# Two of the four weight-block sums of each summed unit are made by GpSimd instead of VectorE

## The chip, the core and the metric

The kernel runs on one core of one Trainium2 chip. A core has five engines that run their own instruction streams and meet only at semaphores: TensorE (PE, the matmuls; PEld is its weight load), VectorE (DVE), ScalarE (ACT), GpSimd (POOL) and SyncE (SP, which here only issues DMAs). The metric is the device time of one execution in microseconds. Three executions of the kernel before took 2109.12, 2109.4 and 2110.14 us; the median is 2109.4.

## The reference, cut to what matters

Two decoder layers over 256 tokens of width 2048: an RG-LRU and dilated attention mixer, then an MLP; a differential attention mixer, then an MLP. All arrays are float32. The change touches only the MLPs:

```python
def squared_relu_mlp(x, w1, w2):      # w1: 2048 x 8192, w2: 8192 x 2048
    h = jax.nn.relu(x @ w1)
    return (h * h) @ w2
x = layer_norm(ALPHA * x + squared_relu_mlp(x, mlp_w1[layer], mlp_w2[layer]), ...)
```

## The kernel before, in words

**Three products for one.** Each float32 operand is cut in two: a rounded part "hi" (ScalarE copies it to fp32r) and the rest "lo" (VectorE subtracts hi from the original). A product is then three matmuls, hi by hi, hi by lo and lo by hi (`three_products`, lines 1101 to 1103). So every weight that arrives by DMA passes through ScalarE and then VectorE before TensorE can use it.

**The turns.** An MLP takes its 16 strips of 512 hidden columns in pairs. The first pair and the last strips are made apart; the other six pairs are six *turns* (`pair_step`), five in a hardware loop and one behind it. There are twelve turns in the kernel, six in each layer. A turn first multiplies x by two strips of w1 (the up half), then turns and squares the hidden values and multiplies an earlier pair by w2 (the down half, 16 chunks). The up half consists of eight *units* of 1 MB of w1 each: two K tiles by two strips, which is four blocks of 128x512, in the order w_12, w_11, w_22, w_21. `UNITS = "SSOSOSSO"`: units 0, 1, 3, 5 and 6 are *summed*, the others ordinary.

**A summed unit** uses seven block products instead of eight, as in Strassen's scheme. Three work on blocks as they came (`plain_products`, 9 matmuls), four on sums of blocks (`summed_products`, 12 matmuls). The sums are T_1 = w_12 - w_11 and T_3 = w_12 - w_22 (one instruction, line 2046, 128x1024), then T_2 = w_22 - T_1 and T_4 = w_21 - T_2 (two instructions, line 2050, 128x512 each). T_4 needs T_2, and T_2 needs T_1. The four sums lie in `w_sums[e % 2]`, which is the tile `late` for the summed units 0, 3 and 6 and part of `rg` for units 1 and 5.

**The path of a summed unit, number u.** The DMA lands. VectorE makes the four sums (`weight_sums`, parts 0, 1, 2). ScalarE makes hi of the three plain blocks (`plain_hi`, line 860) and, when all four sums are there, hi of the sums (`summed_hi`, line 868). VectorE makes lo of the plain blocks in place in `raw` (`plain_lo`, line 2023), which must wait until the last sum has read them, and then lo of the sums in place (`summed_lo`, line 2030). TensorE waits for `s_plain_lo` before the plain and for `s_lo` before the summed products. Ordinary units and the down half have a simpler path: `chunk_hi` (line 854), `chunk_lo` (line 2010), two chunks of 128x1024 a unit.

**What sets the order.** Nothing is scheduled by a program: each engine's order is the order of the calls in its own `pair_step`. Weights land in four slots (`raw`) used in a ring; the lo parts are made in place there, so the load of a unit (SP, line 417) waits on `s_used` until TensorE has used the unit four before it, and for a summed one until its plain products are done. SP also issues small DMAs that move turned blocks (line 411) in between. VectorE adds finished down products to the residual in the same queue (`add_down`, line 1608), which waits for TensorE.

**GpSimd** does almost nothing: a memset and small loads at the start, four pairs of loads of the gain and bias rows of the layer norms (line 533) and, at the very end, part of the last layer norm (lines 539 and 541). The lines to follow are quoted here:

Of the kernel before, what the change touches and what calls it, by code (L numbers as in the profile page):

```python
# [34 lines left out]
P = 128  # L35
# [169 lines left out]
def build(nc, x, positions, ev_w_in, ev_conv_w, ev_conv_b, ev_gate_a_w, ev_gate_a_b, ev_gate_x_w,  # L205
# [12 lines left out]
    with ExitStack() as ctx:  # L218
# [3 lines left out]
        def sem(name):  # L222
            return ctx.enter_context(nc.semaphore(name))
# [106 lines left out]
        s_sums, s_sum_hi, s_sum_lo = sem("x_sums_made"), sem("x_sums_hi"), sem("x_sums_lo")  # L330
        s_wsum = sem("weight_sums_made")
        s_relu = sem("hidden_cut_at_zero")
        s_plain_hi, s_plain_lo = sem("plain_blocks_hi"), sem("plain_blocks_lo")
        s_prod, s_copied, s_final = sem("products_joined"), sem("first_product_copied"), sem("pair_completed")
        s_dve, s_pool = sem("vector_step"), sem("gpsimd_step")
# [21 lines left out]
        def raw_unit(k):  # L357

            q = k % BLK // 2
            return raw[:, 2 * q:2 * q + 2].rearrange("p k t c -> p (k t c)")  # L360

        def sum_cell(j, e, h):

# [141 lines left out]
        def _(pool):  # L505
# [16 lines left out]
                    pool.dma_start(gates_w[64 * half:64 * half + 64, n, :, 64 * half:64 * half + 64], src).then_inc(s_gw, 16)  # L522


            for n in range(4):
                if n == 0:
                    pool.wait_ge(s_yalo, 2)
                elif n == 2:
                    pool.wait_ge(s_gained, GROUPS * n)
                else:  # L530
                    pool.wait_ge(s_used, ((B_M0, B_M1)[n // 2] + 2 * FB - 2) * BLK)
                for i, row in enumerate(ln_rows(n)):
                    pool.dma_start(gain_bias[:, i], row.partition_broadcast(P)[:, 0, :]).then_inc(s_gb, 16)
# [11 lines left out]
        def _(act):  # L545
# [279 lines left out]
            def mlp(n, b0):  # L825
# [37 lines left out]
                def summed_hi(blk, u, turn):  # L863

                    e = SUMMED.index(u)
                    act.wait_ge(s_wsum, turn * (3 * NS) + (3 * e + 3))
                    act.wait_ge(s_used, blk * BLK + (RING_PRIOR[2 * u + 1] + 1))
                    nc.scalar.activation(hi_part(RING_CELL[2 * u + 1], 4), w_sums[e % 2], ACT.Copy).then_inc(s_hi, 2)

# [637 lines left out]
        def _(dve):  # L1507
# [478 lines left out]
            def mlp(n, b0, n0):  # L1986
# [32 lines left out]
                def plain_lo(blk, u, turn):  # L2019

                    dve.wait_ge(s_plain_hi, turn * NS + (SUMMED.index(u) + 1))
                    dve.wait_ge(s_wsum, turn * (3 * NS) + (3 * SUMMED.index(u) + 3))
                    nc.vector.tensor_tensor(lo_part(2 * u, 1, 3), raw_unit(2 * u)[:, CN:4 * CN],
                                            hi_part(RING_CELL[2 * u], 3).bitcast(F32), ALU.subtract).then_inc(s_plain_lo, 1)

# [4 lines left out]
                    nc.vector.tensor_tensor(w_sums_lo[e % 2], w_sums[e % 2], hi_part(RING_CELL[2 * u + 1], 4).bitcast(F32),  # L2030
                                            ALU.subtract).then_inc(s_lo, 2)

                def weight_sums(blk, u, turn, part):

                    e = SUMMED.index(u)
                    w_12, w_11, w_22, w_21 = (raw_unit(2 * u)[:, j * CN:j * CN + CN] for j in range(4))
                    t = [w_sums[e % 2][:, j * CN:j * CN + CN] for j in range(4)]
                    if part == 0:  # L2040
                        dve.wait_ge(s_raw[u % PAIRS], (blk + u // PAIRS) * 16)
                        if e >= 2:
                            dve.wait_ge(s_used, blk * BLK + (2 * SUMMED[e - 2] + 2))
                        pair = w_sums[e % 2][:, 0:2 * CN].rearrange("p (a c) -> p a c", a=2)
                        w_2, w_1 = (raw_unit(2 * u).rearrange("p (a c) -> p a c", a=4)[:, a:b] for a, b in ((0, 1), (1, 3)))
                        nc.vector.tensor_tensor(pair, w_2.to_broadcast([P, 2, CN]), w_1, ALU.subtract).then_inc(s_wsum, 1)
                    else:
                        dve.wait_ge(s_wsum, turn * (3 * NS) + (3 * e + part))
                        out, a, b = ((t[T_2], w_22, t[T_1]), (t[T_4], w_21, t[T_2]))[part - 1]
                        nc.vector.tensor_tensor(out, a, b, ALU.subtract).then_inc(s_wsum, 1)  # L2050

                def add_down(blk, q, nb, k):

# [83 lines left out]
                def pair_step(i, last=False):  # L2137
# [5 lines left out]
                    def lo(k):  # L2143
                        chunk_lo(blk, k, RING_CELL[k])

                    def sums(u, part):
                        weight_sums(blk, u, turn, part)

                    sums(0, 0)
                    add_down(blk, i, 2, -4)  # L2150
                    sums(0, 1)
                    sums(0, 2)
                    plain_lo(blk, 0, turn)
                    sums(1, 0)
                    summed_lo(blk, 0)
                    sums(1, 1)
                    sums(1, 2)
# [3 lines left out]
                    sums(3, 0)  # L2161
                    lo(4)
                    sums(3, 1)
                    lo(5)
                    sums(3, 2)
                    plain_lo(blk, 3, turn)
                    summed_lo(blk, 3)
                    sums(5, 0)
                    lo(8)
                    sums(5, 1)  # L2170
                    lo(9)
                    sums(5, 2)
                    plain_lo(blk, 5, turn)
                    sums(6, 0)
                    summed_lo(blk, 5)
                    sums(6, 1)
                    sums(6, 2)
                    plain_lo(blk, 6, turn)
                    summed_lo(blk, 6)
                    lo(14)  # L2180
# [172 lines left out]
```

## Time and profile before

| | |
|---|---|
| median of three executions | 2109.4 us |
| the profiled execution, its own time | 2108.34 us |
| its span, first to last instruction | 2106.6 us |
| TensorE busy | 2087.9 us, 99% |
| VectorE busy | 1628.7 us, 77% |
| ScalarE busy | 1098.6 us, 52% |
| GpSimd busy | 25.6 us, 1% |
| granted TensorE clock, mean | 0.998 |

The span is 1.74 us shorter than the execution's own time, and that execution is 1.06 us below the median. A timeline row merges neighbours that are alike; its duration runs from the first start to the last end. The row of a matmul is 0.39 us long but the next starts 0.227 us after it, since they overlap in the array; the pace is read from the starts. Likewise one VectorE instruction starts some 0.08 us before the one ahead of it has ended.

### The profile page before, as it was taken

Reading aid. Unit: us, or ns where it says so; the run is one execution under the profiler, and the core shown is the slowest. Engines: PE = TensorE matmul, PEld = TensorE weight load, DVE = VectorE, ACT = ScalarE, POOL = GpSimd, SP = SyncE. Lnnn points to the kernel's source line nnn. Section 1 sums busy time; section 2 is a strip of 40 time slices with the busy share of each in tenths; the row PEclk is TensorE's granted clock in tenths of the full one; section 3 lists DMA queues with packets and bytes.
Section 4 is the critical chain, followed back from the end, with each engine's and each line's share of the span. In section 5 each row is a group of like instructions: output and inputs, shape, how many; then the busy total and the mean of one; then the engine's idle time right before and its main releaser. Section 6 shows DMA issues by size and latency. Waiting matters only on the chain.

```text
span 2106.6 us, 26918 instructions
## 1 busy us (share of the span) xinstructions
PE 2087.9 (99%) x9824; PEld 1747.5 (83%) x9824; DVE 1628.7 (77%) x1647; ACT 1098.6 (52%) x1246; POOL 25.6 (1%) x38
## 2 busy tenths in 40 slices
PE   9999999999999999999999999999999999999997
PEld 8888887888888888888888888888888888888886
DVE  6766667869789798896687767577698978978866
ACT  5445656445555455454645554555354554645643
POOL 2000000000000000000000000000000000000001
PEclk9999999999999999999999999999999999999999
DMA  9554574566666666667564555454666666676664
GB/s 288 184 177 160 169 247 164 185 205 211 219 210 227 208 205 217 208 220 272 166 221 159 181 178 179 162 198 155 207 218 209 213 222 203 211 229 198 228 202 178
DMA packets 216122, 426.19 MB, mean 202 GB/s; under 512 B 14992, under 2 KB 50048, under 8 KB 215024
## 3 DMA queue, kind: packets, MB, share of 16 engines
q1 hardware_dynamic: 214208, 415.75, 59.6%
q0 software_dynamic: 1840, 9.44, 1.3%
q8 instruction: 48, 0.79, 0.2%
q14 instruction: 26, 0.21, 0.0%
HBM read 406.26 MB, written 2.10 MB: 194 GB/s over the span
## 4 chain that ended last, share of the span: by engine, by line
PE 96%; DVE 1%; DMA 1%; ACT 1%; POOL 0%; issue 0%; POOLq 0%; ACTq 0%
PE ps L1101 20%; PE ps L1103 20%; PE ps L1102 20%; PE ps L1013 10%; PE ps L1039 6%; PE ps L1041 6%; PE ps L1040 6%; PE ps L1017 5%; DMA raw<-in_ev_w_in 1%; PE ps L1214 0%; PE ps L1084 0%; PE ps L1255 0%; PE ps L1213 0%; PE ps L1218 0%; DVE w_lo L1513 0%
## 5 line engine op out<-in xcount | busy, mean ns | idle before, releaser
L1513 DVE TENSOR_TENSOR w_lo<-raw,w_hi 128x1024 fp32r<-128x1024 f32 x264 | 319.5, 1218 | 126.0 <-ACT w_hi L554 125.2
L1102 PE MATMUL ps<-raw_lo,yT 128*128 128x512 f32 x944 | 367.2, 389 | 0.0
L554 ACT ACTIVATE w_hi<-raw 128x1024 fp32r<-128x1024 f32 x256 | 267.5, 1056 | 169.9 <-PE ps L1041 114.0
L1013 PE MATMUL ps<-xT,w_hi 128*128 128x512 f32 x1016 | 258.7, 396 | 1.4 <-DVE xT L1558 1.0
L854 ACT ACTIVATE w_hi<-raw 128x1024 fp32r<-128x1024 f32 x168 | 173.7, 1050 | 144.7 <-DMA raw<-in_mlp_w 82.7
L1102 PE MATMUL ps<-raw_lo,xT 128*128 128x512 f32 x548 | 213.2, 389 | 0.0
L1013 PEld LDWEIGHTS ps<-xT,w_hi 128*128 128x128 f32 x1016 | 183.1, 188 | 35.6 <-issue 1.5
L1102 PEld LDWEIGHTS ps<-raw_lo,yT 128*128 128x128 f32 x944 | 177.2, 188 | 36.7
L1101 PE MATMUL ps<-w_hi,yT 128*128 128x512 f32 x508 | 198.0, 390 | 0.1
L1103 PE MATMUL ps<-w_hi,yT 128*128 128x512 f32 x508 | 197.7, 389 | 0.0
L854 ACT ACTIVATE more_hi<-raw 128x1024 fp32r<-128x1024 f32 x116 | 116.8, 1050 | 127.5 <-DMA raw<-in_mlp_w 127.5
L2010 DVE TENSOR_TENSOR raw_lo<-raw,w_hi 128x1024 fp32r<-128x1024 f32 x136 | 164.6, 1217 | 18.9 <-ACT w_hi L854 18.3
L2010 DVE TENSOR_TENSOR raw_lo<-raw,more_hi 128x1024 fp32r<-128x1024 f32 x116 | 138.4, 1211 | 36.8 <-ACT more_hi L854 36.8
L1101 PE MATMUL ps<-more_hi,yT 128*128 128x512 f32 x380 | 147.8, 389 | 0.0
L1103 PE MATMUL ps<-more_hi,yT 128*128 128x512 f32 x380 | 147.8, 389 | 0.0
L1017 PEld LDWEIGHTS ps<-xT,w_lo 128*128 128x128 f32 x1016 | 136.0, 190 | 8.6 <-DVE w_lo L1513 0.4
L1017 PE MATMUL ps<-xT,w_lo 128*128 128x256 f32 x1016 | 142.6, 284 | 0.2 <-DVE w_lo L1513 0.2
L2010 DVE TENSOR_TENSOR raw_lo<-raw,w_lo 128x1024 fp32r<-128x1024 f32 x76 | 90.5, 1218 | 58.3 <-ACT w_lo L854 58.2
L1101 PE MATMUL ps<-w_lo,yT 128*128 128x512 f32 x336 | 130.9, 390 | 0.5 <-DVE raw_lo L2010 0.5
L1103 PE MATMUL ps<-w_lo,yT 128*128 128x512 f32 x336 | 130.7, 389 | 0.0
L1102 PEld LDWEIGHTS ps<-raw_lo,xT 128*128 128x128 f32 x548 | 102.9, 188 | 21.4
L1101 PE MATMUL ps<-w_hi,xT 128*128 128x512 f32 x304 | 118.3, 389 | 0.0
(300 smaller groups left out, 4059.2 us busy)
## 6 DMA issues: line engine op xcount, KB each, us to landing
raw<-in_mlp_w SPq DMA_DIRECT2D x256, 1024.0 KB, 5.4
raw<-in_od_w_in SPq DMA_DIRECT2D x48, 1024.0 KB, 5.1
raw<-in_ev_w_in SPq DMA_DIRECT2D x36, 1024.0 KB, 5.1
raw<-in_ev_w_out SPq DMA_DIRECT2D x16, 1024.0 KB, 5.1
raw<-in_od_w_out SPq DMA_DIRECT2D x16, 1024.0 KB, 5.1
ks<-cross SPq DMA_DIRECT2D x256, 32.0 KB, 3.8
ks<-qs SPq DMA_DIRECT2D x256, 32.0 KB, 4.2
raw<-in_ev_w_in SPq DMA_DIRECT2D x8, 512.0 KB, 8.3
```

The lines of the kernel that those rows point to most:

```text
L554: nc.scalar.activation(flat(w_hi[:, k % NSPL]), flat(raw[:, k % NRAW]), ACT.Copy).then_inc(s_hi, 1)
L854: nc.scalar.activation(hi_part(cell, 2), flat(raw[:, k % NRAW]), ACT.Copy).then_inc(s_hi, 1)
L1013: return nc.tensor.matmul(ps[:, f], w_hi[:, k % NSPL, i, f * P:f * P + P], both, start=k == 0 and i == 0, stop=k == BLK - 1 and i == CK - 1)
L1017: return nc.tensor.matmul(ps[:, f, S:2 * S], w_lo[:, k % NSPL, i, f * P:f * P + P], xT[:, CK * k + i, 0], start=False, stop=False)
L1039: nc.tensor.matmul(bank, src[:, kt + i, 0, toks], hi, start=(start and i == 0), stop=False)
L1040: nc.tensor.matmul(bank, src[:, kt + i, 0, toks], lo, start=False, stop=False)
L1041: ins = nc.tensor.matmul(bank, src[:, kt + i, 1, toks], hi, start=False, stop=(stop and i == CK - 1))
L1101: nc.tensor.matmul(out, act[0], hi, start=start, stop=False)
L1102: nc.tensor.matmul(out, act[0], lo, start=False, stop=False)
L1103: return nc.tensor.matmul(out, act[1], hi, start=False, stop=stop)
L1513: nc.vector.tensor_tensor(flat(w_lo[:, k % NSPL]), flat(raw[:, k % NRAW]), flat(w_hi[:, k % NSPL]).bitcast(F32), ALU.subtract).then_inc(s_ ...
L2010: nc.vector.tensor_tensor(lo_part(k, 0, 2), flat(raw[:, k % NRAW]), hi_part(cell, 2).bitcast(F32), ALU.subtract).then_inc(s_lo, 1)
```

## The change

In each of the twelve turns and for each of the five summed units, GpSimd makes T_2 and T_4. VectorE still makes T_1 and T_3 in one instruction. GpSimd waits for that instruction (`s_wsum`, now raised once a unit), makes T_2, waits for its own semaphore and makes T_4; both raise the new semaphore `s_later`. `summed_hi` on ScalarE and `plain_lo` on VectorE wait for `s_later` in place of `s_wsum`. GpSimd runs the six turns of a layer as a loop ahead of the load of the gain and bias rows of that layer's second norm. VectorE's list is written anew as well: the first sum of units 1 and 5 now stands earlier in it.

```diff
+            def later_sums(turn):
+                for u in SUMMED:
+                    e = SUMMED.index(u)
+                    t, (_, _, w_22, w_21) = sums_and_blocks(u)
+                    pool.wait_ge(s_wsum, turn * NS + (e + 1))
+                    nc.gpsimd.tensor_tensor(t[T_2], w_22, t[T_1], ALU.subtract).then_inc(s_later, 1)
+                    pool.wait_ge(s_later, turn * (2 * NS) + (2 * e + 1))
+                    nc.gpsimd.tensor_tensor(t[T_4], w_21, t[T_2], ALU.subtract).then_inc(s_later, 1)
+
             for n in range(4):
+                if n % 2 == 1:
+                    with pool.Fori(0, PAIRED - 2) as i:
+                        later_sums(i + (n // 2) * (PAIRED - 2))
...
                 def summed_hi(blk, u, turn):
...
-                    act.wait_ge(s_wsum, turn * (3 * NS) + (3 * e + 3))
+                    act.wait_ge(s_later, turn * (2 * NS) + (2 * e + 2))
...
                 def plain_lo(blk, u, turn):
...
-                    dve.wait_ge(s_wsum, turn * (3 * NS) + (3 * SUMMED.index(u) + 3))
+                    dve.wait_ge(s_later, turn * (2 * NS) + (2 * SUMMED.index(u) + 2))
...
-                    sums(0, 0)
+                    weight_sums(blk, 0)
                     add_down(blk, i, 2, -4)
-                    sums(0, 1)
-                    sums(0, 2)
+                    weight_sums(blk, 1)
                     plain_lo(blk, 0, turn)
-                    sums(1, 0)
                     summed_lo(blk, 0)
...
```

VectorE's queue in the looped turn, before, from `add_down` behind unit 1 to the sums of unit 5. A row is the line, the instruction, its tiles and shape, and the semaphores it waits for; `late_lo` and `rg_lo` are the lo parts of the sums, `raw_lo` those of the blocks as they came.

```order
L2046 TENSOR_TENSOR late<-raw 128x1024 [waits chunk_multiplied,raw_pair_3_loaded]
L2009 REGISTER_ALU
L2010 TENSOR_TENSOR raw_lo<-raw,more_hi 128x1024 [waits w_hi_made]
L2048 REGISTER_ALU
L2050 TENSOR_TENSOR late<-raw,late 128x512 [waits weight_sums_made]
L2009 REGISTER_ALU
L2010 TENSOR_TENSOR raw_lo<-raw,more_hi 128x1024 [waits w_hi_made]
L2048 REGISTER_ALU
L2050 TENSOR_TENSOR late<-raw,late 128x512 [waits weight_sums_made]
...
L2030 TENSOR_TENSOR late_lo<-late,w_hi 128x2048 [waits w_hi_made]
L2041 ISA
L2046 TENSOR_TENSOR rg<-raw 128x1024 [waits chunk_multiplied,raw_pair_1_loaded]
```

The same place after:

```order
L2059 TENSOR_TENSOR late<-raw 128x1024 [waits chunk_multiplied,raw_pair_3_loaded]
L2027 REGISTER_ALU
L2028 TENSOR_TENSOR raw_lo<-raw,more_hi 128x1024 [waits w_hi_made]
L2027 REGISTER_ALU
L2028 TENSOR_TENSOR raw_lo<-raw,more_hi 128x1024 [waits w_hi_made]
L2039 REGISTER_ALU
L2040 REGISTER_ALU [waits plain_blocks_hi]
L2041 TENSOR_TENSOR raw_lo<-raw,more_hi 128x1536 [waits later_weight_sums_made]
L2054 ISA
L2059 TENSOR_TENSOR rg<-raw 128x1024 [waits chunk_multiplied,raw_pair_1_loaded]
L2047 REGISTER_ALU
L2048 TENSOR_TENSOR late_lo<-late,w_hi 128x2048 [waits w_hi_made]
```

The two sums of 128x512 are gone, and the first sum of unit 5 (the `rg` row) stands ahead of the lo part of unit 3's sums instead of behind it. In GpSimd's queue the new work of the first two units of a turn is:

```order
L536 TENSOR_TENSOR late<-raw,late 128x512 [waits weight_sums_made]
L537 ISA
L538 TENSOR_TENSOR late<-raw,late 128x512 [waits later_weight_sums_made]
L535 REGISTER_ALU
L536 TENSOR_TENSOR rg<-raw,rg 128x512 [waits weight_sums_made]
L537 REGISTER_ALU
L538 TENSOR_TENSOR rg<-raw,rg 128x512 [waits later_weight_sums_made]
```

Nothing of this kind stood on GpSimd before; ten such instructions a turn are added, each with a wait.

## Rows read from the trace of the kernel before

**Rows 1.** The page, part 1: busy us, share of the span, instructions.
```profile
PE 2087.9 (99%) x9824; PEld 1747.5 (83%) x9824; DVE 1628.7 (77%) x1647; ACT 1098.6 (52%) x1246; POOL 25.6 (1%) x38
```

**Rows 2.** Busy time by stretch: the second turn of layer 0.
```profile
562.70:646.40 83.70, 83.70 (x371) 69.30 (x370) 71.53 (x61) 44.74 (x40) 0.00 (x0) 1.00 0.65 213
```

**Rows 3.** Who waited for whom, whole span: TensorE for the lo parts.
```profile
PE ps L1101 <- DVE raw_lo L2010: 0.5, 2, 0.3
```

**Rows 4.** Timeline of TensorE: the first matmul of each products group.
```profile
562.71 0.39 PE L1101 MATMUL ps<-w_hi,xT 128*128 128x512 f32 x1
...
567.47 0.39 PE L1101 MATMUL ps<-w_lo,xT 128*128 128x512 f32 x1
...
569.51 0.39 PE L1101 MATMUL ps<-w_lo,yT 128*128 128x512 f32 x1
...
579.71 0.39 PE L1101 MATMUL ps<-w_hi,yT 128*128 128x512 f32 x1
...
592.63 0.39 PE L1101 MATMUL ps<-more_hi,xT 128*128 128x512 f32 x1
...
594.67 0.39 PE L1101 MATMUL ps<-more_hi,xT 128*128 128x512 f32 x1
```

**Rows 5.** Timeline of VectorE, same turn; brackets: idle before, and its releaser.
```profile
555.27 1.76 DVE L2023 TENSOR_TENSOR raw_lo<-raw,w_hi 128x1536 fp32r<-128x1536 f32 x1
557.02 1.23 DVE L2046 TENSOR_TENSOR rg<-raw 128x1024 f32<-128x1024 f32 x1
558.16 2.29 DVE L2030 TENSOR_TENSOR late_lo<-late,w_hi 128x2048 fp32r<-128x2048 f32 x1
...
562.91 1.23 DVE L1608 TENSOR_TENSOR res<-ps,res 128x1024 f32<-128x1024 f32 x1 [1.14 <-PE ps L1103]
...
565.72 2.29 DVE L2030 TENSOR_TENSOR rg_lo<-rg,w_lo 128x2048 fp32r<-128x2048 f32 x1
568.09 1.23 DVE L2046 TENSOR_TENSOR late<-raw 128x1024 f32<-128x1024 f32 x1
569.23 1.22 DVE L2010 TENSOR_TENSOR raw_lo<-raw,more_hi 128x1024 fp32r<-128x1024 f32 x1
...
574.98 2.29 DVE L2030 TENSOR_TENSOR late_lo<-late,w_hi 128x2048 fp32r<-128x2048 f32 x1 [0.40 <-ACT w_hi L868]
...
588.37 1.76 DVE L2023 TENSOR_TENSOR raw_lo<-raw,more_hi 128x1536 fp32r<-128x1536 f32 x1
590.53 2.29 DVE L2030 TENSOR_TENSOR late_lo<-late,more_hi 128x2048 fp32r<-128x2048 f32 x1 [0.40 <-ACT more_hi L868]
```

**Rows 6.** Timeline of ScalarE, same turn.
```profile
557.23 1.47 ACT L860 ACTIVATE w_lo<-raw 128x1536 fp32r<-128x1536 f32 x1
561.94 1.92 ACT L868 ACTIVATE w_lo<-rg 128x2048 fp32r<-128x2048 f32 x1 [3.23 <-DVE rg L2050]
```

**Rows 7.** Timeline of SP: the load of unit 5 is issued.
```profile
569.86 0.39 SPq L417 DMA_DIRECT2D raw<-in_mlp_w  x1
```

**Rows 8.** DMA issues from 549 to 640 us: count, KB each, us to landing.
```profile
raw<-in_mlp_w SPq DMA_DIRECT2D x17, 1024.0 KB, 5.2
```

**Rows 9.** VectorE's later sums, 470 to 970 us, by form: busy, mean ns.
```profile
L2050 DVE TENSOR_TENSOR late<-raw,late 128x512 f32<-128x512 f32 x36 | 24.7, 686 | 0.4
```

**Rows 10.** GpSimd by form, whole span.
```profile
L539 POOL TENSOR_TENSOR res<-res,rg 128x512 f32<-128x512 f32 x1 | 1.3, 1271 | 0.0
```

**Rows 11.** Timeline of the span's end, GpSimd and then VectorE.
```profile
2098.95 1.54 POOL L541 TENSOR_TENSOR res<-res,rg 128x640 f32<-128x640 f32 x1
...
2099.74 1.28 DVE L1710 SCALAR_TENSOR_TENSOR res<-res,tiny,ps 128x1024 f32<-128x1024 f32 x1
```

**Rows 12.** VectorE, 700 to 1500 us, by form, no GpSimd work beside it.
```profile
L1602 DVE SCALAR_TENSOR_TENSOR res<-rg,res 128x1024 f32<-128x1024 f32 x8 | 9.8, 1226 | 0.3
L2271 DVE SCALAR_TENSOR_TENSOR late<-ps,tiny,sub_g 128x256 f32<-128x256 f32 x16 | 7.0, 478 | 0.3
L1584 DVE TENSOR_TENSOR xT<-ks,xT 128x256 fp32r<-128x256 f32 x8 | 3.4, 422 | 4.4 <-ACT xT L630 4.3
```

More of the change, by code:

```diff
@@ L332, in build @@
         s_relu = sem("hidden_cut_at_zero")
+        s_later = sem("later_weight_sums_made")
         s_plain_hi, s_plain_lo = sem("plain_blocks_hi"), sem("plain_blocks_lo")
@@ L360, in raw_unit, with sums_and_blocks @@
             return raw[:, 2 * q:2 * q + 2].rearrange("p k t c -> p (k t c)")
+        def sums_and_blocks(u):
+            t = [w_sums[SUMMED.index(u) % 2][:, j * CN:j * CN + CN] for j in range(4)]
+            return t, [raw_unit(2 * u)[:, j * CN:j * CN + CN] for j in range(4)]
         def sum_cell(j, e, h):
@@ L2031, in summed_lo, with weight_sums @@
                                             ALU.subtract).then_inc(s_lo, 2)
-                def weight_sums(blk, u, turn, part):
+                def weight_sums(blk, u):
                     e = SUMMED.index(u)
[L2038 to L2050, printed above, removed]
+                    dve.wait_ge(s_raw[u % PAIRS], (blk + u // PAIRS) * 16)
+                    if e >= 2:
+                        dve.wait_ge(s_used, blk * BLK + (2 * SUMMED[e - 2] + 2))
+                    pair = w_sums[e % 2][:, 0:2 * CN].rearrange("p (a c) -> p a c", a=2)
+                    w_2, w_1 = (raw_unit(2 * u).rearrange("p (a c) -> p a c", a=4)[:, a:b] for a, b in ((0, 1), (1, 3)))
+                    nc.vector.tensor_tensor(pair, w_2.to_broadcast([P, 2, CN]), w_1, ALU.subtract).then_inc(s_wsum, 1)
                 def add_down(blk, q, nb, k):
@@ L2144, in lo @@
                         chunk_lo(blk, k, RING_CELL[k])
-                    def sums(u, part):
-                        weight_sums(blk, u, turn, part)
-                    sums(0, 0)
+                    weight_sums(blk, 0)
                     add_down(blk, i, 2, -4)
-                    sums(0, 1)
-                    sums(0, 2)
+                    weight_sums(blk, 1)
                     plain_lo(blk, 0, turn)
-                    sums(1, 0)
                     summed_lo(blk, 0)
-                    sums(1, 1)
-                    sums(1, 2)
                     add_down(blk, i, 3, 0)
@@ L2160, in pair_step @@
                     summed_lo(blk, 1)
-                    sums(3, 0)
+                    weight_sums(blk, 3)
                     lo(4)
-                    sums(3, 1)
                     lo(5)
-                    sums(3, 2)
                     plain_lo(blk, 3, turn)
+                    weight_sums(blk, 5)
                     summed_lo(blk, 3)
-                    sums(5, 0)
                     lo(8)
-                    sums(5, 1)
                     lo(9)
-                    sums(5, 2)
                     plain_lo(blk, 5, turn)
-                    sums(6, 0)
+                    weight_sums(blk, 6)
                     summed_lo(blk, 5)
-                    sums(6, 1)
-                    sums(6, 2)
                     plain_lo(blk, 6, turn)
```

## The prediction, made before the changed kernel ran

> **What bounds the kernel now.** I read the page's first part first: TensorE is busy 99% of the span, VectorE 77%, GpSimd 1% [rows 1]. A span that TensorE fills can shrink only where TensorE waits, so the next view is busy time by stretch. In a turn of the MLP TensorE is busy for all of the 83.70 us, VectorE for 71.53 and GpSimd for nothing [rows 2]. The view of who waited for whom has for TensorE in the turns one kind of entry, 0.5 us in two waits for a lo part of line 2010 [rows 3]. So VectorE, relieved or not, is not what sets the time of a turn. What matters is how late the lo parts of a summed unit are ready against the matmul that wants them. That is read by laying two timelines side by side, TensorE's first matmul of each group of products [rows 4] and the end of the lo part that it waits for [rows 5]:
>
> - unit 1: summed lo from 565.72 to 568.01, wanted at 569.51: 1.5 us to spare;
> - unit 3: summed lo from 574.98 to 577.27, wanted at 579.71: 2.4 us;
> - unit 6: plain lo ready at 588.37 + 1.76 = 590.13, wanted at 592.63: 2.5 us; summed lo ready at 590.53 + 2.29 = 592.82, wanted at 594.67: 1.85 us.
>
> The reader is to see that the cover is 1.5 to 2.5 us a unit, and that the order around it does not grow it: a slot of `raw` is loaded when TensorE has used it, so a unit has a fixed time from load to use.
>
> **What is removed.** Two VectorE sums of 128x512 a unit, 0.686 us each [rows 9]: in a turn 10 x 0.686 = 6.9 us, in twelve turns 82 us of VectorE. None of it lies on the path that sets the end, so its removal is worth at most the 0.5 us of waits.
>
> **What is added.** Ten GpSimd sums a turn. The nearest row is a GpSimd tensor_tensor of the same shape with both inputs in SBUF, 1.271 us [rows 10]; the pair of a unit is then 2.54 us against 1.37, plus handoffs that I put at 0.1 to 0.15 us (a wait between two engines costs that in these timelines). By itself this makes a unit's sums ready about 1.3 us later after its first sum; VectorE uses that time for its other lo parts, since 0.686 us twice has left its queue.
>
> **What is moved.** The first sum of unit 1 now stands ahead of `plain_lo` of unit 0. It waits for unit 1's load; before, it began at 557.02 [rows 5], as ScalarE's plain hi of the same unit did at 557.23 [rows 6]. So plain lo of unit 0 moves from 555.27 to about 558.3 and ends at 560.0, with 562.71 wanted: covered. The first sum of unit 5 now stands ahead of summed lo of unit 3. Its load is issued at 569.86 [rows 7] and takes 5.2 us [rows 8], so it lands near 575.1; the sum ends at 576.3, and unit 3's summed lo at about 578.4 instead of 577.27, 1.3 us before it is wanted. Both moves are covered, if nothing else delays VectorE. Behind unit 1, `add_down` still waits for TensorE until 562.91 [rows 5], so an earlier VectorE gains nothing there. GpSimd's queue moves no load: the gain and bias rows behind the loop wait for a TensorE step that lies after the turns anyway.
>
> **The cost that the trace doesn't show: a GpSimd sum beside a VectorE subtraction with both operands in SBUF.** At the end of the span the two engines do run side by side: GpSimd's 128x640 takes 1.54 us while VectorE's 128x1024 takes 1.28 [rows 11]. That VectorE form carries a scalar from memory, which costs 478 - 422 = 56 ns at equal width, and 1226 + 56 = 1282 ns is what it takes alone [rows 12]: neither is slowed. But there VectorE reads one tensor from PSUM. In the turn nearly every VectorE instruction reads two tensors from SBUF (lines 2010, 2023, 2030, 2046), and they fill most of the 71.5 us. So the bounds are: below, nothing (the end of the span), above, that the two never overlap: VectorE stands still for 1.27 us at each GpSimd sum, and GpSimd first waits out the VectorE instruction that is running, up to 2.29 us. I take the upper one, because the row that shows no cost is of a different pairing in just the one respect that this change makes frequent.
>
> The Trainium skill says this of the pairing: "A DVE instruction with two SBUF inputs contends with a GpSimd instruction that reads SBUF" (SBUF — State Buffer, Who interferes with whom), and that whoever starts first holds the shared ports for its whole instruction. By that rule the chain below holds; by the rows of the span's end alone the sum would be nothing. No row of this trace has the pairing itself.
>
> **The chain, if they exclude each other** (VectorE by the spacing of its starts, 1.13 us for 1024 columns, 1.68 for 1536, 2.20 for 2048; ScalarE 1.8 for the sums, 1.4 for the plain blocks; GpSimd 1.27; handoffs 0.1). In the second turn, by its clock:
>
> Unit 1: first sum ends 558.2; VectorE goes straight on with plain lo of unit 0 to 560.0, so T_2 runs 560.0 to 561.3, summed lo of unit 0 to 563.5 (wanted 564.75), T_4 to 564.8. ScalarE's summed hi ends 566.7, summed lo 569.0, wanted 569.51: 0.5 left of 1.5. Unit 3: its first sum ends 570.1, chunk 4 at 571.3, T_2 at 572.5, chunk 5 at 573.7, T_4 at 574.9, plain lo 576.7, unit 5's first sum 577.8, summed lo 580.1 with 579.71 wanted: TensorE waits 0.43. Unit 5: T_2 581.3, chunk 8 582.5, T_4 583.8, chunk 9 584.9, plain lo 586.6, unit 6's first sum 587.7, summed lo of unit 5 589.9: just in time. Unit 6: T_2 591.2, T_4 592.5, plain lo 594.3, wanted 592.63 + 0.43 = 593.06: 1.3 late. Summed lo 596.8, wanted by then at 596.4: 0.4 late. Sum: 0.43 + 1.31 + 0.4 = 2.1 us a turn. The down half has no sums and catches up, so each turn starts even: 12 x 2.14 = 25.7 us, and since TensorE has no idle time in a turn, none of it is taken back. Span 2106.6 + 25.7 = 2132.3; with the 1.74 us around it 2134.0; the profiled execution was 1.06 below the median, so 2135.
>
> The slope matters more than the point: from the moment TensorE waits, the eight GpSimd pieces of units 1, 3, 5 and 6 lie in one chain, so each tenth of a microsecond in a piece is 0.8 us a turn and 10 us in all. At 1.05 us a piece the waits are gone; at 1.6 they are 4.8 a turn.
>
> **Rivals.**
> 1. *Not slower: the engines overlap freely.* For it: the end of the span [rows 11, 12]. Then the latest point is unit 3's summed lo, 1.3 us early as worked out above; unit 1's is as before, unit 6's earlier. TensorE never waits; time 2109.4. This case also takes in sharing so mild that a piece costs VectorE less than about 1.0 us. It decides against my forecast at the point where TensorE shows no wait at lines 1101 to 1103 in the turns.
> 2. *Exclusion, and GpSimd's sums are longer too* (a piece of 1.6 us, by being interrupted or by the wait's register work). 12 x 4.8 = 57 us: 2167. Against it: in the row the same shape needs 1.27, and one wait in front of it.
> 3. *Faster.* The freed 6.9 us of VectorE a turn removes TensorE's waits for lo parts. All there is to win is 0.5 us [rows 3]: 2108.9, not to be told from no change. For more TensorE's pace itself would have to rise, and it is even at 0.227 us whether VectorE is busy or idle.
>
> **How the numbers follow.** Exclusion near the row's duration (my forecast, 2115 to 2160 as its own range): 0.48. No or mild contention: 0.40. Exclusion with longer pieces: 0.09. Faster for a reason not seen: 0.03. A measurement of this kernel tells a change from none at about 0.2%, 4 us. Slower by more: nearly all of 0.57, less 0.01 for a sum below 4 us: 0.56. Faster 0.03, same 0.41. The likeliest case gives 2135. The range must reach down to the unchanged time and up to most of the long pieces: 2108 to 2160.
>
> **What would show it.** In the changed kernel's profile: GpSimd busy 120 x 1.27 = 152 us more if its rows carry the sums alone, more if its waits for the ports are in them. If VectorE's lines for 1024 and 2048 columns keep 1.22 and 2.29 us, there is no exclusion and the forecast falls; if some of them grow by a microsecond, it stands. TensorE's waits should be at unit 3's and unit 6's lo parts in the up half, none in the down half, and turns 85 to 86 us apart. Wrong in another way: a longer turn without waits of TensorE, or waits at unit 0, which I count as covered.

## The result: 20.6 us slower, and the profile after

The changed kernel takes 2129.8 us (median of 4 runs, 2129.0 to 2130.6) where the kernel before took 2109.3 on the same chip (2108.1 to 2110.1): a ratio of 1.0098, 95% interval 1.0085 to 1.0111. 2135 was forecast, in a range of 2108 to 2160. The profiled execution has a span of 2128.5 us against 2106.6 (mean granted clock 0.998).

The page's part 1 of the kernel after answers to [rows 1]:

```profile
PE 2098.9 (99%) x9824; PEld 1743.9 (82%) x9824; DVE 1601.8 (75%) x1527; ACT 1098.2 (52%) x1246; POOL 300.5 (14%) x158
```

VectorE has 120 instructions fewer and should have lost 120 x 0.686 = 82 us [rows 9]. It lost 27. So its other instructions grew by about 55 us. GpSimd has 120 more, and grew by 275 us instead of 152: its rows hold more than the sums.

The second turn of layer 0 by busy time, the answer to [rows 2] (same columns), shows 85.50 us in which TensorE was busy for 84.59:

```profile
565.00:650.50 85.50, 84.59 (x371) 69.19 (x370) 69.23 (x52) 44.64 (x39) 22.94 (x11) 1.00 0.63 209
```

How far apart the turns are tells more than the idle time, since a matmul's end is modelled: its row is longer than the way to the next start, and that of a late one shows 0.50 us instead of 0.39. The first matmul of unit 0's products starts at 564.99, 650.32, 735.78 and 821.28 us in three successive turns, 85.43 apart; before, at 562.71, 646.35 and 729.99, 83.64 apart. That is 1.79 us a turn, and 12 turns make 21.5 of the 21.9 us by which the span grew. Where in a turn they arise, the view of who waited for whom says (us in total, times, longest), first for TensorE's matmuls and then for its weight loads, which is the answer to [rows 3]:

```profile
PE ps L1119 <- DVE raw_lo L2041: 6.8, 12, 0.6
PE ps L1119 <- DVE late_lo L2048: 3.8, 12, 0.4
...
PEld ps L1119 <- DVE late_lo L2048: 12.5, 23, 0.8
PEld ps L1119 <- DVE raw_lo L2041: 11.9, 12, 1.1
```

Twelve turns, twelve waits for a plain lo, that of unit 6, and 23 for a summed lo: unit 6's in every turn, unit 3's in eleven. TensorE's timeline of the same turn places them (brackets: idle before, and its releaser), and answers to [rows 4]:

```profile
581.78 0.39 PE L1121 MATMUL ps<-more_hi,yT 128*128 128x512 f32 x1
582.02 0.50 PE L1119 MATMUL ps<-w_hi,yT 128*128 128x512 f32 x1
582.35 0.40 PE L1120 MATMUL ps<-late_lo,yT 128*128 128x512 f32 x1
...
594.87 0.39 PE L1121 MATMUL ps<-w_lo,xT 128*128 128x512 f32 x1
595.81 0.50 PE L1119 MATMUL ps<-more_hi,xT 128*128 128x512 f32 x1 [0.56 <-DVE raw_lo L2041]
596.15 0.39 PE L1120 MATMUL ps<-raw_lo,xT 128*128 128x512 f32 x1
...
598.50 0.50 PE L1119 MATMUL ps<-more_hi,xT 128*128 128x512 f32 x1 [0.35 <-DVE late_lo L2048]
598.84 0.39 PE L1120 MATMUL ps<-late_lo,xT 128*128 128x512 f32 x1
```

Matmuls start 0.227 us apart when nothing is late. At unit 3's summed products the steps are 0.24 and 0.33, which is 0.1 too long; at unit 6's plain products 0.94 and 0.34, 0.8 too long; at unit 6's summed products, by the same reading, 0.6. Of each of these, 0.11 is in the second step, to a matmul whose lo part is ready by then; so it is behind all 35 waits. All three places lie in the up half. The down half (607.80 to 650.50) is filled, and starts late by what the up half lost.

**Why the lo parts are late.** VectorE's timeline of this turn answers to [rows 5]:

```profile
559.36 1.22 DVE L2059 TENSOR_TENSOR rg<-raw 128x1024 f32<-128x1024 f32 x1 [3.12 <-DMA raw<-in_mlp_w]
560.50 1.75 DVE L2041 TENSOR_TENSOR raw_lo<-raw,w_hi 128x1536 fp32r<-128x1536 f32 x1
562.16 3.38 DVE L2048 TENSOR_TENSOR late_lo<-late,w_hi 128x2048 fp32r<-128x2048 f32 x1
565.47 1.21 DVE L1626 TENSOR_TENSOR res<-ps,res 128x1024 f32<-128x1024 f32 x1
...
572.24 3.45 DVE L2028 TENSOR_TENSOR raw_lo<-raw,more_hi 128x1024 fp32r<-128x1024 f32 x2
576.87 1.76 DVE L2041 TENSOR_TENSOR raw_lo<-raw,more_hi 128x1536 fp32r<-128x1536 f32 x1 [1.18 <-POOL late L538]
...
581.88 4.55 DVE L2028 TENSOR_TENSOR raw_lo<-raw,w_hi 128x1024 fp32r<-128x1024 f32 x2
594.00 1.76 DVE L2041 TENSOR_TENSOR raw_lo<-raw,more_hi 128x1536 fp32r<-128x1536 f32 x1 [2.56 <-POOL late L538]
596.15 2.29 DVE L2048 TENSOR_TENSOR late_lo<-late,more_hi 128x2048 fp32r<-128x2048 f32 x1 [0.39 <-ACT more_hi L886]
```

and GpSimd's of the same time, which was empty before:

```profile
555.18 1.30 POOL L536 TENSOR_TENSOR late<-raw,late 128x512 f32<-128x512 f32 x1 [46.57 <-DVE late L2059]
...
560.66 2.74 POOL L536 TENSOR_TENSOR rg<-raw,rg 128x512 f32<-128x512 f32 x1 [2.80 <-DVE rg L2059]
563.48 3.23 POOL L538 TENSOR_TENSOR rg<-raw,rg 128x512 f32<-128x512 f32 x1
...
589.32 3.28 POOL L536 TENSOR_TENSOR late<-raw,late 128x512 f32<-128x512 f32 x1 [3.96 <-DVE late L2059]
592.67 1.29 POOL L538 TENSOR_TENSOR late<-raw,late 128x512 f32<-128x512 f32 x1
```

The two are read together. GpSimd's sum at 560.66 comes while VectorE's 1.75 us subtraction has just begun; it waits that one out (to 562.25) and ends 1.15 us later, at the start of VectorE's next: the 2048-column subtraction shows 3.38 us where it needs 2.29. It stood still for 1.09. GpSimd's next, at 563.48, has to wait until that subtraction ends at 565.5, and then shows 3.23; VectorE's `add_down` beside it (L1626, one operand in PSUM) keeps its 1.21. A sum that VectorE has nothing against shows 1.29. Over the whole span the shortest sum is 1.29 us and the longest 3.28, and two VectorE rows together (x2, 4.55) can hold two standstills, 2.36 + 2 x 1.09. The turn has four: in the rows at 562.16 and 572.24 and two in that at 581.88. That is 4.4 us, and 52 in twelve turns, of the 55 by which VectorE's instructions grew. The other six GpSimd sums of the turn fall beside nothing of this kind, or VectorE is waiting for them.

Who waits for GpSimd itself shows too: plain lo of unit 3 for 1.18 us, that of unit 6 for 2.56, the two sums of unit 6 one behind the other. VectorE has nothing queued ahead of plain lo then that it could do.

### The profile page after: what moved, and what is told of

Same layout as the page of the kernel before. It is cut to its first block, busy times and chain, and to the rows that moved or that the text cites. A ratio compares the mean times of both kernels' runs of the same rounds, so it can differ in the third digit from the quotient of the medians.

```text
span 2128.5 us, 26974 instructions
## 1 busy us (share of the span) xinstructions
PE 2098.9 (99%) x9824; PEld 1743.9 (82%) x9824; DVE 1601.8 (75%) x1527; ACT 1098.2 (52%) x1246; POOL 300.5 (14%) x158
## 4 chain that ended last, share of the span: by engine, by line
issue 62%; PE 21%; POOL 12%; DVE 2%; ACT 1%; DMA 1%; POOLq 0%; DVEq 0%; ACTq 0%
PE ps L1031 6%; POOL late L536 4%; POOL rg L536 3%; POOL rg L538 3%; PE ps L1035 3%; PE ps L1119 3%; PE ps L1120 3%; PE ps L1121 3%; POOL late L538 2%; DMA raw<-in_ev_w_in 1%; PE ps L1057 1%; PE ps L1058 1%; PE ps L1059 1%; DVE w_lo L1531 1%; ACT w_hi L572 0%
## 5 line engine op out<-in xcount | busy, mean ns | idle before, releaser
L536 POOL TENSOR_TENSOR late<-raw,late 128x512 f32<-128x512 f32 x36 | 81.3, 2259 | 1205.6 <-DVE late L2059 1205.6
L2028 DVE TENSOR_TENSOR raw_lo<-raw,w_hi 128x1024 fp32r<-128x1024 f32 x136 | 189.9, 1410 | 17.0 <-ACT w_hi L872 17.0
L2028 DVE TENSOR_TENSOR raw_lo<-raw,more_hi 128x1024 fp32r<-128x1024 f32 x116 | 150.5, 1325 | 36.6 <-ACT more_hi L872 36.4
```

The costliest lines, as they stand in the source:

```text
L536: nc.gpsimd.tensor_tensor(t[T_2], w_22, t[T_1], ALU.subtract).then_inc(s_later, 1)
L2028: nc.vector.tensor_tensor(lo_part(k, 0, 2), flat(raw[:, k % NRAW]), hi_part(cell, 2).bitcast(F32), ALU.subtract).then_inc(s_lo, 1)
```

## The experiments

My theory: a GpSimd instruction that reads SBUF and a VectorE instruction with two SBUF operands exclude each other, and the standstills carry through to TensorE. Rivals: the order of VectorE's queue, the longer path of the sums through GpSimd and back without any standstill, a gain from the relieved VectorE, and something about GpSimd's work apart from its reads. Times are medians with ratios to the kernel before on the same chip.

**The order alone.** Before, with the first sums of units 1 and 5 moved ahead as the change has them:

```diff
                     sums(0, 2)
-                    plain_lo(blk, 0, turn)
                     sums(1, 0)
+                    plain_lo(blk, 0, turn)
 ...
-                    summed_lo(blk, 3)
                     sums(5, 0)
+                    summed_lo(blk, 3)
```

> VectorE makes all sums as before; only the first sum of unit 1 stands ahead of plain lo of unit 0, and the first sum of unit 5 ahead of summed lo of unit 3, as in the changed kernel. Exclusion theory (the 20.6 us come from GpSimd's sums and VectorE's two-operand instructions standing still for each other): no change, 2109 us within 4. Order theory (the wait for a load in front of a ready lo part is what makes TensorE wait): most of the 20 us is here, 2120 to 2130.

Measured: 2110.25 us, 1.0008 (0.9999 to 1.0017). The order costs about 1.8 of the 20.6 us; the interval goes from 0 to 3.6. By the starts of the matmuls 1.5 us of it lie in one place, at the summed products of unit 0 in seven of the twelve turns, where TensorE waits for `add_down`:

```profile
647.31 1.22 DVE L1608 TENSOR_TENSOR res<-ps,res 128x1024 f32<-128x1024 f32 x1
...
648.67 0.49 PE L1101 MATMUL ps<-w_hi,yT 128*128 128x512 f32 x1 [0.20 <-DVE res L1608]
```

**The relief alone.** After, with both GpSimd sums replaced by short writes, so that T_2 and T_4 are left out. GpSimd's loop over the turns is written out too, here and in the runs with two writes and with one operand; the other runs keep the loop:

```diff
-                    nc.gpsimd.tensor_tensor(t[T_2], w_22, t[T_1], ALU.subtract).then_inc(s_later, 1)
+                    nc.gpsimd.memset(t[T_2], 1.0).then_inc(s_later, 1)
 ...
-                    nc.gpsimd.tensor_tensor(t[T_4], w_21, t[T_2], ALU.subtract).then_inc(s_later, 1)
+                    nc.gpsimd.memset(t[T_4], 1.0).then_inc(s_later, 1)
```

> The changed kernel, but in place of T_2 and T_4 GpSimd writes a constant there with a memset of 128x512 (some 0.5 us, no read), so two of the four sums are left out; all waits stay. Exclusion theory: VectorE's rows keep 1.22 and 2.29 us, TensorE has no waits in the turns, 2109 us within 4: the removed 6.9 us of VectorE a turn are worth nothing. Order theory: 2120 to 2130. Relief theory (a freer VectorE gains time where nothing stands against it): below 2105.

Measured: 2110.05 us, 1.0006 (0.9997 to 1.0015), with a memset at 0.53 us. 82 us less work on VectorE, and less delay on the sums than before, are worth nothing that can be measured. That settles the rival "faster".

**The collision alone.** Before, all sums still on VectorE; GpSimd makes ten subtractions a turn of a constant's columns into a scratch tile, for which nobody in the turns waits (one more stands ahead of them, and VectorE waits for GpSimd once, behind the turns of a layer):

```diff
+            def shadow_sums(turn):
+                for u in SUMMED:
+                    e = SUMMED.index(u)
+                    pool.wait_ge(s_later, turn * (2 * NS) + (2 * e + 1))
+                    pool.wait_ge(s_wsum, turn * (3 * NS) + (3 * e + 1))
+                    nc.gpsimd.tensor_tensor(shadow, cst[:, 0:CN], cst[:, 384:384 + CN], ALU.subtract).then_inc(s_later, 1)
+                    pool.wait_ge(s_later, turn * (2 * NS) + (2 * e + 2))
+                    nc.gpsimd.tensor_tensor(shadow, cst[:, 0:CN], cst[:, 384:384 + CN], ALU.subtract).then_inc(s_later, 1)
 ...
```

> The kernel before, with ten extra GpSimd subtractions of 128x512 a turn into a tile nobody reads, each pair released by the first sum of a unit; nobody waits for them but GpSimd. VectorE still makes all sums. Exclusion theory: VectorE loses 1.1 us at each, 11 us a turn, on top of its full load; by the chain of the turn TensorE then waits some 6 us a turn: 2185 us, range 2150 to 2200. Longer-path theory (the loss comes from the sums being ready late, since a GpSimd sum takes 1.3 us and a handoff): nothing waits for these sums, so 2109.

Measured: 2198.6 us, 1.0424 (1.0408 to 1.044): 90 us slower, by instructions whose result no one in the turns wants. VectorE's later sums and GpSimd's subtractions by form (busy us, mean ns), and TensorE's two longest kinds of wait:

```profile
L2069 DVE TENSOR_TENSOR late<-raw,late 128x512 f32<-128x512 f32 x36 | 50.7, 1409 | 0.4
...
L531 POOL TENSOR_TENSOR sm<-cst 128x512 f32<-128x512 f32 x60 | 147.3, 2455 | 1191.4 <-DVE late L2065 1060.7
...
PE ps L1120 <- DVE raw_lo L2042: 26.1, 12, 2.2
PE ps L1120 <- DVE res L1627: 18.1, 12, 2.2
```

The sum that needs 0.686 us [rows 9] takes 1.409 on average. The collision needs neither shared data nor a VectorE that waits for GpSimd.

**The path alone.** After, each sum replaced by two writes, together as long as a sum (0.747 + 0.527 us); T_2 and T_4 are left out:

```diff
-                    nc.gpsimd.tensor_tensor(t[T_2], w_22, t[T_1], ALU.subtract).then_inc(s_later, 1)
+                    nc.gpsimd.memset(sm[:], 0.0).then_inc(s_step, 1)
+                    pool.wait_ge(s_step, turn * (2 * NS) + (2 * e + 1))
+                    nc.gpsimd.memset(t[T_2], 0.5).then_inc(s_later, 1)
 ...
```

> The changed kernel, but each of GpSimd's sums is replaced by two memsets, 128x768 into a tile nobody reads and 128x512 into the sum's place, about 1.2 us with the wait between them and no read; T_2 and T_4 are left out. A piece takes GpSimd about as long as the sum did in the kernel before's end (1.27 us). Exclusion theory, with reads as what collides: no VectorE row grows, 2109 us within 4. Longer-path theory: as the changed kernel, 2125 to 2130. If writes collide as well, VectorE's rows grow and the time lies between.

Measured: 2108.85 us, 1.0002 (0.9993 to 1.0011). VectorE by form, 470 to 970 us, first of the kernel after, then of this one:

```profile
L2028 DVE TENSOR_TENSOR raw_lo<-raw,w_hi 128x1024 fp32r<-128x1024 f32 x54 | 77.9, 1461 | 0.0
```
```profile
L2033 DVE TENSOR_TENSOR raw_lo<-raw,w_hi 128x1024 fp32r<-128x1024 f32 x54 | 64.9, 1219 | 2.5 <-ACT w_hi L877 2.4
```

1461 ns against 1219. The handoffs, the pair of 2.5 us and the new order are all still there, and VectorE waits for GpSimd ahead of the plain lo of units 3 and 6 (7.0 us in 12 waits, six turns); next to none of it reaches TensorE. This is the run that decides: when GpSimd only writes, nothing is left of the change's cost that can be measured. The Trainium skill's rule (SBUF — State Buffer, Who interferes with whom) says that an instruction with two SBUF inputs on VectorE contends with a GpSimd one that reads SBUF, "not with one that only writes it"; by that rule this run and the one with the shadow sums come out as they did, and the trace agrees, with 1.219 us on average in a kernel whose GpSimd only writes.

**One operand read instead of two.** After, each sum replaced by a scaling of the weight block, so that T_2 and T_4 are left out:

```diff
-                    nc.gpsimd.tensor_tensor(t[T_2], w_22, t[T_1], ALU.subtract).then_inc(s_later, 1)
+                    nc.gpsimd.tensor_scalar(t[T_2], w_22, 0.5, None, ALU.mult).then_inc(s_later, 1)
 ...
-                    nc.gpsimd.tensor_tensor(t[T_4], w_21, t[T_2], ALU.subtract).then_inc(s_later, 1)
+                    nc.gpsimd.tensor_scalar(t[T_4], w_21, 0.5, None, ALU.mult).then_inc(s_later, 1)
```

> The changed kernel, but GpSimd's two sums are replaced by a multiplication of w_22 and of w_21 by 0.5 (one SBUF input instead of two, 128x512, written to the sum's place), so two of four sums are left out. Theory that any GpSimd read collides with VectorE's second read: VectorE's rows still grow, by the time such a piece reads, which I put at 0.4 to 0.7 us (half the reads of the sum's 1.1); under 1.05 us a piece TensorE has no waits: 2109 within 4. Theory that only two-input GpSimd instructions collide: no row grows, also 2109. The time will not tell these apart, VectorE's rows will.

Measured: 2116.6 us, 1.0038 (1.0024 to 1.0052). The time was missed, the standstill is at the low end of what was expected. Timelines of GpSimd and VectorE around unit 0's summed lo:

```profile
553.90 1.49 POOL L536 TENSOR_SCALAR late<-raw 128x512 f32<-128x512 f32 x1 [46.53 <-DVE late L2059]
...
559.38 2.94 POOL L536 TENSOR_SCALAR rg<-raw 128x512 f32<-128x512 f32 x1 [2.41 <-DVE rg L2059]
```
```profile
560.88 2.70 DVE L2048 TENSOR_TENSOR late_lo<-late,w_hi 128x2048 fp32r<-128x2048 f32 x1
```

VectorE stands 2.70 - 2.29 = 0.41 us for a piece that lasts 1.49 alone, and GpSimd still waits out the VectorE instruction in front. I had not reckoned with the piece itself being 0.2 us longer than a sum; the pair of unit 6, which VectorE and TensorE wait for, is 0.4 longer, and its summed lo is up to 0.45 late. The run changes the kind of instruction along with the number of operands, so that the second operand alone makes the difference between 0.41 and 1.09 is not shown.

**Fewer units on GpSimd.** A tuple says which units' sums GpSimd makes; the others' stay on VectorE, interleaved with its lo parts as in the kernel before, and the order of the first sums is the change's. Without unit 6:

```diff
+        BY_POOL, BY_DVE = (0, 1, 3, 5), (6,)
```

> The changed kernel, but VectorE makes T_2 and T_4 of unit 6 itself, where it made them before; GpSimd has units 0, 1, 3 and 5. Exclusion theory, by the chain of the turn: TensorE's two waits at unit 6 (1.8 of the 2.0 us of its weight-load waits in a turn) go, and the one at unit 3 stays at 0.1 to 0.3 us a turn: 2110 to 2113 us. If the loss were spread evenly over the units (each unit's pair costs a fifth of 20.6 us) it would be 2126.

Measured: 2116.3 us, 1.0036 (1.0023 to 1.005), where 2110 to 2113 was expected. TensorE's wait for the plain lo of unit 6 is gone, and with it 13.5 of the 20.6 us. Left are 24 waits for summed lo parts, of units 3 and 6 (weight loads, us in total, times, longest):

```profile
PEld ps L1128 <- DVE late_lo L2057: 9.7, 24, 0.7
```

Without units 3 and 6:

```diff
+        BY_POOL, BY_DVE = (0, 1, 5), (3, 6)
```

> GpSimd has units 0, 1 and 5; VectorE makes the sums of 3 and 6. Exclusion theory: the VectorE rows beside the six GpSimd sums still grow by 1.1 us, but each is used up by the 1.5 to 2.9 us to spare, TensorE has no waits in the turns: 2109 within 4. Even-spread theory: 3/5 of 20.6 us, 2121.

Measured: 2112.7 us, 1.002 (1.0011 to 1.0029), with 11 waits of 3.8 us in all on the weight loads. And unit 0 alone, whose sums fall where no collision could be seen:

```diff
+        BY_POOL, BY_DVE = (0,), (1, 3, 5, 6)
```

> GpSimd makes the later sums of unit 0 alone; there VectorE has an addition with one operand in PSUM beside the first piece and then waits for a load. Exclusion theory: no VectorE row grows, the relief of 1.4 us a turn is worth nothing: 2109 within 4, the best that this idea can give. If relief of VectorE had a worth, 2105 or less.

Measured: 2112.3 us, 1.0016 (1.0007 to 1.0025). No VectorE row grows (1024 columns at 1213 to 1220 ns), so this is not the collision. TensorE's starts say what it is. In all twelve turns the summed products of unit 0 come late, as in the run with the order alone, by 2.4 us in all of the 3.3. VectorE makes unit 1's sums ahead of `add_down`, which ends at 565.75 here, and TensorE's steps are 0.25 and 0.34:

```profile
564.53 1.22 DVE L1635 TENSOR_TENSOR res<-ps,res 128x1024 f32<-128x1024 f32 x1
...
565.64 0.39 PE L1130 MATMUL ps<-w_hi,yT 128*128 128x512 f32 x1
565.89 0.49 PE L1128 MATMUL ps<-w_hi,yT 128*128 128x512 f32 x1
566.23 0.40 PE L1129 MATMUL ps<-late_lo,yT 128*128 128x512 f32 x1
```

In the run without units 3 and 6 that place has only 0.5 us; 2.2 us lie at the summed products of units 3 and 6, in steps of at most 0.3, and the rest is spread. The cost falls step by step as units leave GpSimd, and unit 6, the last in the chain, carries most of it.

**The old order with the change.** After, with the first sums of units 1 and 5 put back behind the lo parts:

```diff
-                    weight_sums(blk, 1)
                     plain_lo(blk, 0, turn)
+                    weight_sums(blk, 1)
 ...
-                    weight_sums(blk, 5)
                     summed_lo(blk, 3)
+                    weight_sums(blk, 5)
```

> The changed kernel with the first sums of units 1 and 5 put back behind plain lo of unit 0 and behind summed lo of unit 3. By the chain: the small wait at unit 3 goes (0.1 to 0.3 us a turn), the waits at unit 6 stay, since its sums are still made after two GpSimd pieces beside a busy VectorE: 2125 to 2129 us, against 2130 of the changed kernel. If the new order were what the exclusion needs to do harm, 2109.

Measured: 2134.7 us, 1.012 (1.0104 to 1.0135). I missed this one: the order, which costs a little by itself, wins back about 5 us here. Unit 5's pair starts later, its plain lo at 588.61, and pushes unit 6's first sum to 590.29 and its plain lo from 594.00 to 596.26:

```profile
596.26 1.76 DVE L2041 TENSOR_TENSOR raw_lo<-raw,more_hi 128x1536 fp32r<-128x1536 f32 x1 [2.55 <-POOL late L538]
```

**Only the last sum on GpSimd.** VectorE makes the third right behind the first two:

```diff
+                def second_sum(u, turn):
 ...
+                    dve.wait_ge(s_wsum, turn * (2 * NS) + (2 * e + 1))
+                    nc.vector.tensor_tensor(t[T_2], w_22, t[T_1], ALU.subtract).then_inc(s_wsum, 1)
 ...
                     weight_sums(blk, 1)
+                    second_sum(1, turn)
```

> The changed kernel, but VectorE makes T_2 itself, right behind T_1 and T_3; GpSimd makes T_4 alone, five pieces a turn instead of ten. Exclusion theory by the chain: each unit meets one standstill of 1.1 us and one wait for the running instruction instead of two; what is left fits almost into the 1.5 to 2.5 us to spare: 0 to 0.5 us a turn, 2109 to 2115 us. If the loss were proportional to the number of GpSimd sums: 2119.

Measured: 2120.1 us, 1.0051 (1.0037 to 1.0064), a miss again. Half of the loss or more is in one place of the trace: TensorE waits at unit 0 for `add_down` (L1624). VectorE's timeline, TensorE's matmul, and that kind of wait in all:

```profile
562.82 3.38 DVE L2046 TENSOR_TENSOR late_lo<-late,w_hi 128x2048 fp32r<-128x2048 f32 x1
566.12 1.21 DVE L1624 TENSOR_TENSOR res<-ps,res 128x1024 f32<-128x1024 f32 x1
...
567.48 0.49 PE L1117 MATMUL ps<-w_hi,yT 128*128 128x512 f32 x1 [0.48 <-DVE res L1624]
...
PE ps L1117 <- DVE res L1624: 5.3, 12, 0.6
```

In the kernel before `add_down` ends at 562.91 + 1.23 = 564.14 [rows 5] and TensorE wants it at about 564.7: a margin of 0.6 us that my list of margins left out. To test this, the third sum of unit 1 was moved behind the summed lo of unit 0 (shown against the run above):

```diff
-                    second_sum(1, turn)
                     plain_lo(blk, 0, turn)
                     summed_lo(blk, 0)
+                    second_sum(1, turn)
```

> The kernel with T_4 alone on GpSimd (2120 us), with one line moved: VectorE's T_2 of unit 1 stands behind summed lo of unit 0 instead of ahead of plain lo of unit 0. Its T_4 then falls beside the addition that reads PSUM, and that addition is not pushed past the summed products of unit 0, which wait for it. If that is where the eleven us came from (TensorE's waits for line 1624, 0.6 us a turn and more): those waits go, no VectorE row at unit 0 grows, and the time is 2110 to 2114 us. If the loss is spread over the five GpSimd sums: 2118 to 2120.

Measured: 2114.8 us, 1.003 (1.0019 to 1.0041). Those twelve waits are gone, `add_down` starts at 564.27, and about 5 us come back, about as many as the waits held (11.1 us over the kernel before on the same chip, now 6.3). What stays is at unit 3's summed lo, late in all twelve turns (2.5 us in 6 waits of the matmuls, 7.7 in 12 of the weight loads).

**Smaller pieces.** After, each GpSimd sum cut in two of 128x256:

```diff
-                    nc.gpsimd.tensor_tensor(t[T_2], w_22, t[T_1], ALU.subtract).then_inc(s_later, 1)
+                    nc.gpsimd.tensor_tensor(t[T_2][:, 0:CN // 2], w_22[:, 0:CN // 2], t[T_1][:, 0:CN // 2], ALU.subtract).then_inc(s_later, 1)
+                    pool.wait_ge(s_later, turn * (4 * NS) + (4 * e + 1))
+                    nc.gpsimd.tensor_tensor(t[T_2][:, CN // 2:CN], w_22[:, CN // 2:CN], t[T_1][:, CN // 2:CN], ALU.subtract).then_inc(s_later, 1)
 ...
```

> The changed kernel with each GpSimd sum cut in two of 128x256, one after the other: twenty pieces a turn, the same sums. Theory with queueing (each piece first waits out the VectorE instruction that is running, then holds the port): the standstills add up to as much as before (20 x 0.55 = 11 us), but a unit's sums wait for four VectorE instructions instead of two. By the chain of the turn TensorE waits 4 us a turn: 2157 us, range 2140 to 2165. Theory with the held time alone: as the changed kernel, 2130, or a little less. If GpSimd and VectorE shared the port element by element, 2130 as well.

Measured: 2154.2 us, 1.0217 (1.0201 to 1.0232), within the range that was expected. The cost more than doubles, from 20.6 to 45 us. GpSimd's first halves by form, VectorE's summed lo of unit 0, and GpSimd's timeline at unit 5:

```profile
L536 POOL TENSOR_TENSOR late<-raw,late 128x256 f32<-128x256 f32 x36 | 61.3, 1703 | 1194.3 <-DVE late L2063 1194.3
...
564.33 2.83 DVE L2052 TENSOR_TENSOR late_lo<-late,w_hi 128x2048 fp32r<-128x2048 f32 x1
...
583.07 2.73 POOL L536 TENSOR_TENSOR rg<-raw,rg 128x256 f32<-128x256 f32 x1 [3.01 <-DVE rg L2063]
585.87 1.61 POOL L538 TENSOR_TENSOR rg<-raw,rg 128x256 f32<-128x256 f32 x1
587.55 1.60 POOL L540 TENSOR_TENSOR rg<-raw,rg 128x256 f32<-128x256 f32 x1
```

A half takes 0.74 us alone, and holds VectorE up by 2.83 - 2.29 = 0.54 us, half of a whole sum's 1.09. So the held time alone would have made this kernel no slower. But a piece that comes beside a running VectorE instruction waits it out, and then only half a sum gets done. Twice the pieces don't wait twice as often (by the lengths of GpSimd's rows eight a turn, against seven of the whole sums); what grows is the wait for the sums to be complete: VectorE stands ahead of the plain lo parts for 46.2 us in six turns, where it was 22.6 in the kernel after. The expectation had the time, but not this path to it: it let each unit's sums wait for four VectorE instructions, and here they wait for three at most.

## Why the prediction was right, and where it was off

- **What bounds the kernel.** Right. TensorE fills the turn, and VectorE's relief is worth nothing, by the run with short writes.
- **Exclusion.** Right, and shown from four sides: VectorE rows that grow by 1.09 us or twice that, the shadow sums, none of it beside writes or beside the row with a PSUM operand. The first rival, free overlap, falls by the 3.38 us row; the wait that the detour adds falls by the run with two writes.
- **The size of a standstill.** This is the term that was mis-sized: 1.27 us a piece, taken from the row's length; measured 1.09. About 0.2 us of a GpSimd row don't hold VectorE up. The Trainium skill has the pair held "for the whole instruction" (SBUF — State Buffer, SBUF: two separate sides); by that the standstill would be the row's 1.29, and the trace says 1.09, for a half 0.54 of 0.74, and for one operand read 0.41 of 1.49.
- **The sum over a turn.** Forecast 2.14 us in three waits, 0.43 + 1.31 + 0.4. Measured 1.79 by the distance of the turns; by TensorE's steps about 0.1 + 0.8 + 0.6. Same places, smaller at the first two, larger at the third. Of the sum's 25.7 us, 21.5 came.
- **The slope.** Wrong as put. By "each tenth of a microsecond in a piece is 0.8 us a turn" a standstill of 1.09 would have left 2.14 - 1.8 x 0.8 = 0.7 us a turn, and the turn lost 1.79. Where VectorE is idle and waits for GpSimd, 1.18 us at unit 3 and 2.56 at unit 6, a piece counts with its whole 1.29, so not all eight shrank. With five of them shorter by 0.18 the sum is 1.2. Most of the other 0.6 can be read in the turn shown. Unit 6's summed lo ends at 596.15 + 2.29 = 598.44, 33.45 us behind the turn's start, and was wanted 594.67 - 562.71 = 31.96 behind it: 1.49 late, some 0.25 more than 1.2; 0.2 of that lie between plain lo and summed lo, 2.7 us from end to end where the chain had 2.5, with a wait of 0.39 for ScalarE. TensorE starts 0.06 later still, and the next step is 0.11 too long, which makes 1.66 of this turn's 1.69; other turns lose up to 0.2 more. The chain had put that last step at nothing. Why it costs 0.11 no run shows. The prediction's "at 1.05 us a piece the waits are gone" doesn't follow from its own slope either: 2.14 us at 0.8 a tenth are used up at 1.0.
- **The moves.** Unit 1's first sum ahead and unit 5's ahead were called covered, and alone they cost about 2 us, most of it at unit 0, by the margin of the next point. That together with the change they help by 5 us the prediction did not say.
- **The margin that was missed.** "Waits at unit 0, which I count as covered" held for the kernel after, where `add_down` ends at 565.47 + 1.21 = 566.68 and is wanted 2.04 us behind the turn's start, at 567.03, as in the kernel before; 0.35 us was left. With a VectorE sum of 0.69 us more in front of it (the run with the last sum alone) it was the largest wait; with the shadow sums TensorE waited there for 18.1 us; and it is most of what the order alone and unit 0 alone cost. The list of margins should have held every VectorE result that TensorE waits for, not the lo parts only.
- **The rival with longer pieces** (1.6 us, 2167). GpSimd's rows are 1.29 to 3.28 us, and for a moment that looks like this rival. But the extra is time in which it waits for VectorE, which the chain has already: 2167 did not come.
- **A reading.** The 56 ns that the prediction gives to the scalar from memory compare a row with an operand in PSUM with one without, so they hold both. The instruction that it judges by them has both too, so that it wasn't slowed stands.

No version tried beats the kernel before; those within 0.1% of it change only the order (2110.25 us) or let GpSimd only write (2110.05 and 2108.85).

## What to carry to other kernels

Before moving work from VectorE to GpSimd, look at what runs beside it: against VectorE instructions with two SBUF operands a GpSimd subtraction isn't parallel work, it is put in line with them, at 1.09 us of VectorE for a sum that VectorE itself makes in 0.69. Relieving an engine that TensorE doesn't wait for gains nothing, and any delay is paid where the chain of parts is tightest, so list every margin of the bounding engine first, those of tenths above all. If such a piece has to run there, cutting it shorter made it worse here: the halves held VectorE up half as long each, but the sums were complete later, and the loss grew from 20.6 to 45 us.

## What the runs showed of the hardware that I had not expected

- How long VectorE stands doesn't go by how long GpSimd runs. It was 1.09 us of 1.29 for two operands of 128x512, 0.54 of 0.74 for two of 128x256, 0.41 of 1.49 for one of 128x512, and nothing for writes of 0.53 and 0.75 us. Only pieces that read held it up, and half the columns by half as much; how one operand makes 0.41 these runs don't explain.
- With one operand a GpSimd 128x512 instruction took longer (1.49 us, a multiplication by a constant) than with two (1.29, a subtraction).
- After a wait the clock can fall. In the kernel with the shadow sums TensorE had waited 2.15 us for a lo part; in a stretch behind it the granted clock was 0.56, near the 1.2 GHz level, matmuls started 0.43 us apart instead of 0.227, and each showed 0.63 instead of 0.39. By stretch (TensorE, weight loads, VectorE, ScalarE, GpSimd, clock, DMA share, GB/s), and by timeline:

```profile
516.00:519.50 3.50, 3.50 (x10) 2.71 (x11) 3.30 (x2) 3.50 (x5) 0.00 (x0) 0.56 0.00 0
```
```profile
515.87 0.50 PE L1120 MATMUL ps<-more_hi,xT 128*128 128x512 f32 x1 [2.15 <-DVE raw_lo L2042]
...
517.31 0.63 PE L1121 MATMUL ps<-raw_lo,xT 128*128 128x512 f32 x1
```

  That costs about 8 matmuls x 0.2 = 1.6 us on top of the wait. By the starts of the matmuls it followed eight of the twelve waits at this place, which look alike, and what decides it no run shows. Eight times 1.6 is about 13 us, as much as this kernel's 2198.6 lies above the expected 2185. The kernel after, whose waits stay under 1.1 us, shows 1.00 in the turn above.
